# Rounding the next projection's two panels two attention steps sooner, in mixers B and C of the first layer too

## The reference

```python
px = split_cols(hx @ w_in)          # latents: q, k, v of the mixers A, B, C and a gate
pc = split_cols(hc @ w_in)          # the same for the context
ya, yca = global_gqa(...)           # mixer A: latents over all keys; context over context
yb, ycb = neighbourhood_attn(...)   # mixer B: 2-D neighbourhood with a bias, and the context
yc_, ycc = window_gqa(...)          # mixer C: window of +-128 with a sink logit, and the context
ux = jnp.concatenate([ya, yb, yc_], axis=-1) * jax.nn.silu(px[9])
x = x + gate[:, None, :] * (ux @ w_out)
```

## Time and profile before

| | |
|---|---|
| median of 3 runs | 1872.13 us |
| the profiled execution's own time | 1871.63 us |
| its span, first to last instruction | 1869.8 us |
| TensorE busy | 1842.0 us, 99% |
| VectorE busy | 1262.9 us, 68% |
| ScalarE busy | 1084.1 us, 58% |
| DMA, mean over the span | 153 GB/s |
| granted TensorE clock, mean | 0.996 |
| attention of mixer B, first layer | about 239 to 293 us |
| attention of mixer C, first layer | about 365 to 420 us |

### The profile page before, as it was taken

One profiled execution on the slowest core, in us unless ns is written; L12 is line 12 of the kernel. 1 busy time (PEld: TensorE's weight loads), 2 busy tenths in 40 slices (PEclk: granted clock), 3 DMA queues, 4 the chain that ended last, 5 costly groups with the idle time before them and its releaser, 6 DMA issues.

```text
span 1869.8 us, 33135 instructions
## 1 busy us (share of the span) xinstructions
PE 1842.0 (99%) x12776; PEld 1595.9 (85%) x12776; DVE 1262.9 (68%) x2156; ACT 1084.1 (58%) x1899; POOL 54.5 (3%) x55
## 2 busy tenths in 40 slices
PE   7999999999999999999999999999999999999998
PEld 5878878879888988889889988889888889998887
DVE  6663344467736578786686787767776677687865
ACT  5372264385726477764556567746774555567762
POOL 0000000003000000001000000000000000000001
PEclk9999999999999999999999999999999999999999
DMA  9232243232224214555532454545554642355553
GB/s 356 91 114 88 93 158 113 91 126 101 91 97 163 94 70 176 181 201 201 185 136 91 158 181 181 196 179 186 184 193 172 223 154 91 124 179 191 182 181 134
DMA packets 42566, 285.41 MB, mean 153 GB/s; under 512 B 4944, under 2 KB 6352, under 8 KB 9424
## 3 DMA queue, kind: packets, MB, share of 16 engines
q1 hardware_dynamic: 40832, 278.24, 41.4%
q0 software_dynamic: 1616, 5.52, 0.9%
HBM read 282.69 MB, written 1.05 MB: 152 GB/s over the span
## 4 chain that ended last, share of the span: by engine, by line
PE 94%; DVE 2%; ACT 2%; issue 1%; DMA 1%; SPq 0%; POOL 0%; DVEq 0%; ACTq 0%
PE bank L2297 25%; PE bank L2291 14%; PE bank L2293 13%; PE bank L2292 13%; PE bank L2298 13%; PE bank L2510 4%; PE bank L2542 4%; PE bank L2485 4%; PE bank L2393 1%; PE bank L2463 1%; DMA token_major<-weights 1%; DVE panels_lo L1463 1%; ACT work L1057 1%; PE bank L2535 1%; PE bank L2491 0%
## 5 line engine op out<-in xcount | busy, mean ns | idle before, releaser
L2297 PE MATMUL bank<-acts,panels_hi 128*128 128x512 f32 x2032 | 710.6, 396 | 0.5 <-DVE panels_lo L1463 0.5
L1463 DVE TENSOR_TENSOR panels_lo<-raw_panels,panels_hi 128x1024 fp32r<-128x1024 f32 x468 | 573.5, 1243 | 188.2 <-ACT panels_hi L916 186.6
L916 ACT ACTIVATE panels_hi<-raw_panels 128x1024 fp32r<-128x1024 f32 x468 | 484.0, 1053 | 248.0 <-PE bank L2293 150.8
L2298 PE MATMUL bank<-acts,panels_lo 128*128 128x256 f32 x2032 | 565.3, 278 | 0.0
L2297 PEld LDWEIGHTS bank<-acts,panels_hi 128*128 128x128 f32 x2032 | 381.3, 188 | 91.8 <-DVE panels_lo L1463 1.3
L2298 PEld LDWEIGHTS bank<-acts,panels_lo 128*128 128x128 f32 x2032 | 382.1, 188 | 0.1
L2291 PE MATMUL bank<-acts,panels_hi 128*128 128x256 f32 (+1 forms) x1120 | 350.5, 313 | 0.8 <-DVE xT L1542 0.4
L2292 PE MATMUL bank<-acts,panels_hi 128*128 128x256 f32 (+1 forms) x1120 | 345.7, 309 | 0.0
L2293 PE MATMUL bank<-acts,panels_lo 128*128 128x256 f32 (+1 forms) x1120 | 345.7, 309 | 0.0
L2291 PEld LDWEIGHTS bank<-acts,panels_hi 128*128 128x128 f32 x1120 | 213.5, 191 | 16.6 <-issue 3.9
L2293 PEld LDWEIGHTS bank<-acts,panels_lo 128*128 128x128 f32 x1120 | 213.5, 191 | 10.9
(11 more groups left out here) (299 smaller groups left out, 1865.6 us busy)
## 6 DMA issues: line engine op xcount, KB each, us to landing
raw_panels<-weights SPq DMA_DIRECT2D x252, 1024.0 KB, 4.8
token_major<-weights SPq DMA_DIRECT2D x4, 1024.0 KB, 8.5
near_bias<-rpb POOLq DMA_DIRECT2D x16, 256.0 KB, 3.4
xT<-xin SPq DMA_DIRECT2D x4, 512.0 KB, 5.5
gates<-weights SPq DMA_DIRECT2D x2, 1024.0 KB, 10.1
near_bias<-weights SPq DMA_DIRECT2D x4, 512.0 KB, 7.4
token_major<-weights SPq DMA_DIRECT2D x2, 512.0 KB, 12.8
out<-xT SPq DMA_DIRECT2D x4, 256.0 KB, 2.4
```

What stands on the lines that cost most here:

```text
L916: act.activation(slot_hi(n, a, b), raw_of(n, a, b), ACT.Copy).then_inc(hi_ready, 1)
L1463: dve.tensor_tensor(slot_lo(n, a, b), raw_of(n, a, b), slot_hi(n, a, b).bitcast(F32), ALU.subtract).then_inc(lo_ready, 1)
L2297: pe.matmul(bank.rearrange("p (c t) -> p c t", c=2), whi_, with_rest(xhi_), start=start, stop=False, skip_group_check=True)
L2298: return pe.matmul(bank[:, 0:T], wlo_, xhi_, start=False, stop=stop, skip_group_check=True)
```

## The change

`sooner` becomes 2 for all three mixers of the first layer:

```diff
--- before.py
+++ after.py
@@ -1016,7 +1016,7 @@
             steps, pairs = attention_plan(blk, mixer, with_ctx)
             g0, p0 = st.at["groups"], st.at["pairs"]
             late = late_gate(mixer, st.layer) if blk == 1 else 0
-            sooner = 2 if blk == 1 and mixer == "A" and with_ctx else 0
+            sooner = 2 if blk == 1 and with_ctx else 0
             for i in range(len(steps) + 6):
                 if late and i == 2:
                     act.wait_ge(gate_last, late)
```

## The result

| | before | after |
|---|---|---|
| median | 1872.49 us (1869.28 to 1875.39, 20 runs) | 1875.44 us (1870.92 to 1879.97, 20 runs) |
| profiled execution, its span | 1871.63 us, 1869.8 us | 1878.61 us, 1876.8 us |
| TensorE waits before L2510 for L1039 | 1.5 us, 6 times | 4.3 us, 7 times |

The ratio is 1.0016, 95% interval 1.001 to 1.0023: slower by 0.16%, less than the 0.2% that was taken as no change, but not nothing. In microseconds it is +2.95 between the medians, where +1.73 was forecast.

The account below looks back on a forecast made before the run. TensorE was taken to bound the kernel, so only its waits count. B +0.92 us (+0.95 - 0.03) and C +0.81 us (+0.95 - 0.14) made +1.73 us on 1872.13, forecast 1873.9 us, range 1871.2 to 1876.0.

Parts of the forecast that it names:

- Step 10: ScalarE, i = 10: the first half's 0.95 us rounding costs nothing, covered by waits of 1.34 (B) and 1.45 us (C).
- Step 11: ScalarE, i = 11: the second half's rounding delays the last copy and TensorE's transposes by 0.95 us in each mixer.
- Steps 12 and 13, VectorE: Second panel's roundings take the first's places, no cost; VectorE's earlier splits (maxima 0.2 us later) are covered by ScalarE.
- The gain at the piece: Next projection's start: TensorE's shorter wait for the panel's low parts gives 0.03 us in B, 0.14 us in C.
- DMAs: Weight loads: no cost; the panel lands after the 4.8 us median, at 278.14, 1.1 us before it is needed.
- Rival 4: Mixer B's panel lands late, after up to 9.6 us, adding 3.3 us: 1877.2 us; chance 0.04.
- Rival 1: Nothing moves: the last transposes wait for other things too and TensorE absorbs the shift; 1872.0 us, chance 0.16.
- rival 2: Faster: earlier splits shorten TensorE's waits for low parts and perhaps for the copies, 0.72 us in all; 1871.4 us, chance 0.04.
- rival 3: The rounding at i = 10 also delays a copy, its slack used up; at most 1875.8 us, chance 0.08.

Follow-up runs that it names:

- again: The changed kernel once more without an edit, against the kernel before: 1876.92 us, ratio 1.0018.
- sooner1: The changed kernel with mixers B and C moved one step sooner instead of two, against the kernel before: 1877.26 us, ratio 1.0016.
- skip11: The changed kernel with the first panel's second half rounded at i = 12 instead of 11, against the kernel before: 1873.97 us, ratio 1.0004.
- act_only: ScalarE's roundings moved as in the change, VectorE's splits left in their old places, against the kernel before: 1874.51 us, ratio 1.0003.
- b_only: The change in mixer B alone, C left as before, against the kernel before: 1876.23 us, ratio 1.0016.
- fill0: The kernel before with 6 of the next projection's 12 matmuls ahead of the last transposes, roundings and splits unmoved: 1882.52 us, ratio 1.004.

## Why the prediction was right, and where it was short

The time came out 1.5 us above the forecast and inside its range, 0.6 us below its upper end. The mechanism that carries the +1.73 us, one rounding for each mixer ahead of the last copy, was the forecast one. But the change of the time was +2.95 us, and the forecast mechanism holds 1.8 of it: that the time still fell inside the range is in part the 1 us allowed for the spread of medians, and in part luck. Two signs by which the prediction wanted to be called wrong did come, in C in the first trace: L916 waited for a DMA, and the copy of step 9 had no wait before it. Point by point:

- **Step 10.** Right where the panel is there: the wait before the copy of step 9 went to 0.40 us in B, as worked out (0.39), and to 0.51 in C in again (0.50). In the first trace the panel's own landing used up those 0.50 us.
- **Step 11.** Right. +0.94 to +0.96 us in B; in C +0.95, of which 0.1 came back at the piece. sooner1 and skip11 show that, where the panel is there, this one rounding is the whole of the cost in the tails.
- **Steps 12 and 13, VectorE.** Right: the roundings behind the last copies cost nothing in skip11 either, and act_only gives the same tails with VectorE unmoved.
- **The gain at the piece.** 0.14 us at the start of the piece in C as forecast, 0.10 to 0.12 by its end; about nothing in B.
- **DMAs.** This is the step that failed. It took the median landing of all weight loads for this one, and it compared issue and need for B alone (273.34 and 279.24, 1.1 us to spare). In the trace of before, B's own load (L805, 273 to 274 us) had landed later than the median:

```profile
DMA to landing us min/median/max: 5.6/5.6/5.6
```

  That left 0.3 us and not 1.1. In all 13 traces B's load took 5.3 to 5.9 us, and with two steps sooner it is wanted 5.9 us behind its issue: it was 0.03 us late once (b_only) and never more than 0.6 us early. C has the same time between issue and need: its load was issued at 399.84 in the trace of before and is wanted at 405.71, 5.87 us later. The row of the timeline that shows the issue:

```profile
399.84 0.33 SPq L805 DMA_DIRECT2D raw_panels<-weights  x1
```

  It landed after 4.7 us in before, but after 4.7 to 7.3 us over the 13 traces, and after more than 5.87 us in eight of them. Of the six traces with two steps sooner in C four waited there (1.39, 0.70, 0.27 and 0.25 us), two of them beyond the slack. In each of the four, fifteen DMA engines had reported 4.7 to 4.8 us after the issue and a single one was 1.4 to 2.6 us behind them. Why one engine lags is not shown. Rival 4 was priced as one rare landing of 9.6 us in B; what came is a smaller loss, in C, and more often: (0.87 + 0.17) / 6 = 0.2 us for a launch on these traces.
- **The size.** +1.73 us was forecast, 1.80 us stand in the tails of again, +0.2 us on average come from the panel, and 2.95 to 3.5 us were measured between medians with the whole cost in the tails. The last 1 to 1.7 us are the leftover above, whose cause is open.

Rival 1 fell by every trace that has a rounding at i = 11 (the copy moved and the transposes with it), rival 2 by the missing gain, rival 3 by sooner1: without the rounding at i = 10 the tails are the same. Step 10 counts only where the panel is late beyond the slack, as in C in the first trace.

## What to carry to other kernels

Before moving work earlier on a helper engine, read that engine's idle time ahead of each result that the bound engine waits for: here 1.34 us took a rounding for nothing, and one step later there was none and the same rounding cost its full 0.95 us. An earlier operand brings nothing until the bound engine's order uses it; the move paid only with matmuls put into the wait, and the same matmuls without the move cost 8.4 us. Where a moved step reads a load, take the margin at every place at which it is moved, and take it from the landings of that very load in several traces, not from the median of all loads.

## What the runs showed of the hardware

In fill0 the granted clock of TensorE fell at the end of a wait. Waits and windows of that trace (us, busy time of TensorE, its weight loads, VectorE, ScalarE and GpSimd with instruction counts, granted clock, DMA share, GB/s):

```profile
418.79 0.76 PE L2291 MATMUL bank<-acts,panels_hi 128*128 128x512 f32 x1 [2.58 <-DVE panels_lo L1463]
```

```profile
415.00:418.00 3.00, 1.21 (x18) 0.85 (x16) 2.29 (x7) 2.39 (x5) 0.00 (x0) 1.00 0.03 8
419.00:422.00 3.00, 3.00 (x9) 2.31 (x10) 0.00 (x0) 0.00 (x0) 0.00 (x0) 0.50 0.00 0
423.00:426.00 3.00, 3.00 (x31) 2.32 (x33) 1.13 (x1) 3.00 (x5) 0.00 (x0) 1.00 0.00 0
```

TensorE was idle for 2.58 us, and then ran at 0.50 (1.2 GHz instead of 2.4) although busy all the time. Its matmuls of 128x512 start 0.43 us apart there (419.36 to 419.78), and 0.23 us apart at full clock (424.23 to 424.46). A wait of the same length in B (2.56 us) had no such stretch behind it. The stretch of before at 487.7 us also follows a wait, of 1.8 us, 1.6 us after its end, and the one of sooner1 at 599.3 us follows the wait of 1.92 us. But those at 1525 us in before and 952 us in after follow no wait; TensorE had been busy for over 4 us before each:

```profile
948.00:957.00 9.00, 9.00 (x47) 7.70 (x46) 7.75 (x14) 2.00 (x2) 0.00 (x0) 0.81 0.41 139
```

TensorE is busy for the whole 9 us here, and the mean granted clock is 0.81. So a wait on the bound engine can be followed by a half-clock stretch and then cost more than its length (3.77 us for 2.58 in C of fill0), and such stretches also come without one. With 0 to 3 of them for a launch, at up to 1.6 us each, they are as large as what this change does.
